# A mixture-of-experts transformer layer on one core: the turns of the expert's intermediate rows move behind the next gate/up products

## What is computed

```python
def moe(x, w_router, router_bias, w_gate, w_up, w_down, ws_gate, ws_up, ws_down):
    ...
    def body(acc, blk):
        rows, rw, e = blk
        xb = x_pad[rows]
        h = jax.nn.silu(xb @ w_gate[e]) * (xb @ w_up[e])
        yb = (h @ w_down[e]) * rw[:, None].astype(xb.dtype)
        return acc.at[rows].add(yb), None
    ...
    shared = (jax.nn.silu(xf @ ws_gate) * (xf @ ws_up)) @ ws_down
    return (acc[:T] + shared).reshape(B_, S, D)
```

## Time and profile before

| | us |
|---|---|
| median of 3 runs | 1646.05 (1645.39 to 1646.52) |
| the profiled execution's own time | 1649.41 |
| its span (first to last instruction) | 1647.7 |
| PE busy / PE weight loads busy | 1581.6 / 1313.5 |
| DVE busy | 1188.3 |
| ACT busy | 1031.8 |
| POOL busy | 508.1 |

### The profile page before, as it was taken

How to read it: one execution, slowest core, us unless ns; L and a number is a source line. 1 busy time by engine, 2 the same in 40 slices (tenths; PEclk the granted TensorE clock), 3 DMA queues, 4 the chain that set the end, 5 groups by cost and what they waited for, 6 DMA issues and landing times.

```text
span 1647.7 us, 32186 instructions
## 1 busy us (share of the span) xinstructions
PE 1581.6 (96%) x8246; PEld 1313.5 (80%) x8247; DVE 1188.3 (72%) x2036; ACT 1031.8 (63%) x1705; POOL 508.1 (31%) x495
## 2 busy tenths in 40 slices
PE   6999999999999999899999999999999999999985
PEld 6897888888887788778878888788888887888763
DVE  4214777777777788837777787767777787888857
ACT  3214666666666654427677777666776777778744
POOL 0000000000000135432544465543454444453426
PEclk9999999999999999899999999999999999999995
DMA  7223322222223534568999999999998999999976
GB/s 243 91 80 91 71 49 67 58 64 70 49 66 106 181 119 168 194 203 291 331 297 313 300 366 360 330 288 266 327 322 271 303 348 315 362 366 366 366 242 249
DMA packets 161319, 368.63 MB, mean 224 GB/s; under 512 B 53008, under 2 KB 73488, under 8 KB 161264
## 3 DMA queue, kind: packets, MB, share of 16 engines
q1 hardware_dynamic: 136272, 284.21, 49.4%
q0 software_dynamic: 24992, 83.73, 19.5%
HBM read 294.39 MB, written 65.11 MB: 218 GB/s over the span
## 4 chain that ended last, share of the span: by engine, by line
PE 73%; DVE 7%; DMA 7%; issue 5%; ACT 3%; ACTq 2%; POOL 1%; SPq 0%; DVEq 0%; POOLq 0%
PE bank L1024 6%; PE bank L1030 6%; PE bank L1027 6%; DMA sums_scratch<-ys,sidx 6%; PE q_ps L91 4%; PE q_ps L93 4%; PE q_ps L92 4%; PE out_ps L915 4%; PE k_ps L893 4%; PE out_ps L1083 3%; PE out_ps L1084 3%; PE q_ps L1014 3%; PE k_ps L1051 2%; PE k_ps L1052 2%; PE k_ps L1059 2%
## 5 line engine op out<-in xcount | busy, mean ns | idle before, releaser
L1916 DVE TENSOR_TENSOR gu_lo<-raw_gu,gu_hi 128x1024 fp32r<-128x1024 f32 x260 | 306.4, 1220 | 26.7 <-ACT gu_hi L1395 26.5
L1395 ACT CAST gu_hi<-raw_gu 128x1024 fp32r<-128x1024 f32 x260 | 253.2, 1050 | 3.7 <-DMA raw_gu<-in_moe_w_up_dram 2.8
L1024 PE MATMUL bank<-gu_hi,xb_hi 128*128 128x512 f32 x576 | 234.3, 407 | 5.6 <-DVE gu_lo L1916 4.3
L1027 PE MATMUL bank<-gu_lo,xb_hi 128*128 128x512 f32 x576 | 228.2, 396 | 0.0
L681 POOL DMA_INDIRECT sums_scratch<-ys,sidx x63 | 123.6, 1961 | 155.4 <-DMA sums_scratch<-ys,sidx 121.5
L1916 DVE TENSOR_TENSOR dn_lo<-raw_dn,dn_hi 128x1024 fp32r<-128x1024 f32 x130 | 152.6, 1212 | 3.2 <-ACT dn_hi L1395 2.6
L1030 PE MATMUL bank<-gu_hi,xb_lo 128*128 128x512 f32 x576 | 142.7, 390 | 2.2 <-DVE xb_lo L1920 2.2
L1024 PEld LDWEIGHTS bank<-gu_hi,xb_hi 128*128 128x128 f32 x576 | 110.8, 192 | 29.2 <-issue 6.4
L1395 ACT CAST dn_hi<-raw_dn 128x1024 fp32r<-128x1024 f32 x130 | 129.9, 1051 | 5.0 <-DMA raw_dn<-in_moe_w_down_dram 5.0
L1300 ACT CAST pt_hi<-k_ps 128x512 fp32r<-128x512 f32 (+1 forms) x192 | 85.8, 482 | 75.3 <-PE k_ps L893 74.6
L612 POOL IOTA e<- 128x64 f32 x1 | 0.2, 185 | 429.0 <-DVE xs L1712 429.0
(11 more groups left out here) (305 smaller groups left out, 3982.5 us busy)
## 6 DMA issues: line engine op xcount, KB each, us to landing
raw_gu<-in_moe_w_gate_dram SPq DMA_DIRECT2D x128, 512.0 KB
raw_gu<-in_moe_w_up_dram SPq DMA_DIRECT2D x128, 512.0 KB, 9.2
raw_dn<-in_moe_w_down_dram SPq DMA_DIRECT2D x128, 512.0 KB, 9.0
wqk<-in_fox_w_in_dram SPq DMA_DIRECT2D x66, 128.0 KB, 2.5
v_scratch<-v_out SPq DMA_DIRECT2D x32, 256.0 KB, 2.8
va<-v_scratch SPq DMA_DIRECT2D x16, 512.0 KB, 4.8
fin<-sums_scratch SPq DMA_DIRECT2D x16, 512.0 KB, 8.9
xs<-in_x_dram SPq DMA_DIRECT2D x8, 512.0 KB, 7.6
```

The lines of the kernel that those rows point to most:

```text
L1024: i = pe.matmul(o3, xb_hi[s][:, c], g_hi[:, :, c], start=c == 0, stop=False, skip_group_check=True)
L1027: pe.matmul(o3, xb_hi[s][:, c], g_lo[:, :, c], start=False, stop=False, skip_group_check=True)
L1395: a.copy(hi, raw).then_inc(S[done], 1)
L1916: dve.tensor_tensor(lo, raw, hi, ALU.subtract).then_inc(S[lo_ok], 1)
```

## The change

On PE, `turn_h` moves behind `gate_up`; the wait for `h_ok` alone stays ahead of it. One wait for `ht_lo_ok` in front of `turn_h_further` goes. On ACT, `h_hi` moves behind the four `gu_hi` copies, and on DVE `h_lo` behind the first three `gu_lo` pieces.

```diff
@@ PE, expert
                 with pe.If(before_it > 0):
-                    turn_h(m - 1)
+                    pe.wait_ge(S["h_ok"], m)
                     pe.wait_ge(S["g_lo_ok"], G_PIECES * (e + 2))
                     gate_up(par, w, "rows_", m + 1)
-                    pe.wait_ge(S["ht_lo_ok"], m)
+                    turn_h(m - 1)
                     turn_h_further(xi - 1)
                     turn_next()
                     down_further(par, e + 1, xi - 1)
                 with pe.If(before_it < 1):
-                    turn_h(m - 1)
+                    pe.wait_ge(S["h_ok"], m)
                     pe.wait_ge(S["g_lo_ok"], G_PIECES * (e + 2))
                     gate_up(par, w, "rows_", m + 1)
+                    turn_h(m - 1)
                     turn_next()
@@ ACT, first_half
                     if further_too:
                         further_half(xi - 1)
-                    h_hi(m - 1)
-                    if further_too:
                         further_silu(xi - 1)
                     if pos != "last":
                         next_gate_up(m, e, par)
+                    h_hi(m - 1)
                     if further_too:
                         further_h_hi(xi - 1)
                     silu(m)
@@ DVE, expert
                 with dve.If(before_it > 0):
                     further_sum(xi - 1)
-                    h_lo(m - 1)
                     further_h(xi - 1)
                     next_weights(range(G_PIECES - 1))
+                    h_lo(m - 1)
                     further_h_lo(xi - 1)
...
                 with dve.If(before_it < 1):
+                    next_weights(range(G_PIECES - 1))
                     h_lo(m - 1)
-                    next_weights(range(G_PIECES - 1))
```

## The result

| | before | changed |
|---|---|---|
| median of three runs | 1646.05 us | **1673.12 us** (1672.22 to 1676.19) |
| ratio, with 95% interval | | 1.0166 [1.0149, 1.0182] |
| profiled execution, its span | 1649.41, 1647.7 us | 1672.22, 1670.5 us |

What follows compares the result with a forecast made beforehand. PE, 96% busy, was taken as the bound. Pairs 7.6, late experts 5.5, on-time 2.25, ends 1.6, gain -0.6 made +16.4; two clock falls made +19.8 on the 1646.05 median: 1665 us, range 1655 to 1678.

Steps and rivals of the forecast that it cites:

- The view that decided: Waits view: ACT's four register loads per two-expert pass delay h_hi some 2.1 us, making 13 experts without a block before late.
- The copy at 2.1, down at 2.7: Late expert, us after the group's first turn: ACT's h_hi copy starts at 2.1, PE's down product at 2.7 instead of 0.81.
- The late experts with a block: Six late experts with a further block behind: +1.1 us each, less 0.75 where an odd expert without blocks runs ahead.
- With 0.2 to hand down over: PE's sequencer in late experts: 0.2 us to queue down after its wait ends at 2.5, so register reads end at 5.75.
- Zero's shift of 0.25: The group's first turn comes 0.25 us earlier in the expert: 0.15 of turns and 0.10 of a slow first product.
- The 30 experts with a block before: Gain 0.02 us each, -0.6 in all, nothing lost at L1101; rival of stalls there: +9 us, 1674, chance 0.10.
- The clock: Two falls of PE's clock to half in late experts' longer stalls, 1.7 us each, +3.4; bounds 0 and 22.
- clock falls in most late experts: Rival: thirteen clock falls give 1684 us, six give 1673; chance 0.12 for more than five.
- The ends: First expert +0.5 us, last +1.1, experts 61 and 62 taken as 0 within -2 to +2; 1.6 in the sum.
- The first rival: PE's register reads stay hidden: late experts 0.75 us each, odd ones nothing, +11.4, 1657 or 1658; chance 0.22.
- What was to be seen: Signs: L1051 waits in 13 experts, 1 to 1.9 us; L1073 in 15; gate/up 0.8 after down in odd experts.
- the weight load: Down's first weight load was assumed to wait with its product; loading ahead would save up to 0.15 per restart, 4 us.

Runs made afterwards that it cites:

- e3: The changed kernel with ACT and DVE reading two of four register counts at the head of each pass, the rest behind each expert's first half: 1655.87 us, ratio 1.0071.
- e9: The changed kernel with two more, unused register reads on ACT at the head of each pair of experts: 1707.97 us, ratio 1.0351.
- e10: The changed kernel with two of PE's three register reads moved behind the turns, ahead of the waits for ho and of down: 1678.49 us, ratio 1.0171.
- e11: The changed kernel with both the later ACT and DVE reads of e3 and the moved PE reads of e10: 1662.92 us, ratio 1.0069.
- e5: The kernel before the change, with the same later register reads on ACT and DVE as in e3: 1638.03 us, ratio 0.996.
- e14: The kernel before with later ACT and DVE register reads, the same kernel as e5, run once more: 1636.45 us, ratio 0.9941.
- e2: The changed kernel with PE reading one register at an expert's head, the other two behind gate/up and its wait: 1687.76 us, ratio 1.0261.

## Why the prediction was right or wrong

- **The number** fell inside the range in part by luck. The room up to 1678 had been left for a stall at L1101 or for six falls of the clock. Neither came in the changed kernel. What filled it were costs that the prediction had too small or had not: the hand-over of down, a shift counted twice, and slow reads. The mechanism, late halves of h and reads queued behind their wait, was as predicted.
- **The view that decided** was right: the 2.1 us of "issue" on ACT. e3 removes most of it and the two late groups fall from 19.1 to -1.6 us; e9 makes it longer and they double.
- **The copy at 2.1, down at 2.7**: 2.09 and 2.68. The late experts with a block, predicted 4.35, were 4.2 without the clock.
- **"With 0.2 to hand down over"** is the term that was most too small. From down's last wait to the next gate/up I had 3.2 us; the row of L1048 against that of L1024 gives 4.3 here, of which 0.76 is the two slow reads. The 3.55 that remain are 0.35 more than I had. I took 0.2 from an odd expert in which the sequencer had been free to run; to hand over twelve products with their weights behind a wait takes 0.8 here. The 3.0 for the reads and what follows them, which no row of the prediction shows by itself, was a little too large: 2.7 without the slow reads (933.3 to 936.80, less 0.76).
- **Zero's shift of 0.25 was taken off too often.** It has two parts, 0.10 of a slow first product and 0.15 of turns. For a late or odd expert without a block behind it I compared up to the next gate/up product, which in the kernel before has those same two turns ahead of it. So 0.15 was counted twice, in 14 experts of the middle: some 2 us. The odd expert shows it: zero to gate/up 4.69 against 4.6, yet a loss of 0.77 to 0.97 against 0.6. For experts with a block behind, where I compared up to L1073 or L1083, the same step was right: 0.25 in most of the nine.
- **Slow reads** were not thought of. Expert 12 lost 2.39 and expert 46, with a read of 772 ns, 2.11. The other part of the late group was 0.70 to 1.12 where 0.35 had been predicted: 0.15 and 0.35 of the two points above, and 0.1 because the first product behind a gap is itself slow (0.49 us at 936.80 and 1176.46, against 0.40 for the one at 1163.38 in the earlier trace rows).
- **The 30 experts with a block before**: next to nothing lost at L1101 (two waits, 0.8 us), as taken. Of the gain of 0.6 us only 0.1 is seen. 1.58 from turn to product, to the digit. e9 shows that the bound of 0.3 was no invention: 10.1 us appear there once ACT is later.
- **The clock**: two falls for 3.4 were forecast; four stretches came, at 1.4 each instead of 1.7, 5.7 in all. The rival "clock falls in most late experts" did not come true in the changed kernel (three of the thirteen). It did in e9, with falls in all six late experts with a block; in e10 there were five such experts and in e11 three.
- **The ends**: experts 0 and 1 lost 2.5 and not 1.1 (0.5 and, for expert 1 as an odd one, 0.6); 61 and 62 gave 2.5 back, just outside the -2 to +2. The last stretch gained 2.7 where a loss of 1.1 had been added. These two rows, first of the kernel before, then of the changed one, show why:

```profile
1602.00:1649.00 47.00, 28.11 (x57) 16.12 (x56) 32.51 (x45) 17.74 (x29) 28.03 (x12) 0.50 0.62 246
```

```profile
1649.00:1670.00 21.00, 0.39 (x2) 0.00 (x0) 18.28 (x15) 3.07 (x6) 8.15 (x4) 0.50 0.43 171
```

Before, 28.11 us of PE's work at the end ran at the lower clock; after, 0.39 and a stretch of 3.4 us at 1611.4. The last fall came 47 us later in this profile, 21 us later when counted from the start of the last expert, and this hides part of the loss in the pair. It is scatter and not the change's doing as far as the runs show: e5 and e14, the same kernel, differ by 13 us in this (1597.8 and 1610.9).
- **The first rival** ("reads stay hidden") falls by the 17 waits of L1024 for "issue" and by e2 and e10, in which the odd experts' loss goes away as soon as the reads go elsewhere.
- **What was to be seen**: L1051 waits 9 times and not 13. The prediction's 13 contradicted its own count, since six of the 13 late experts have a block behind them and wait at L1073: there 16, predicted 15. The waits of L1051 are 0.5 to 1.4 us where 1 to 1.9 had been named, the shorter ones behind an odd expert; the idle time before gate/up in the odd experts is 0.64 where 0.8 had been.
- On the weight load: at 932.58 the first load of down's weights and its product start together, behind a wait of 1.39 us. The Trainium skill, "TensorE: Matmul & The Clock Gate", section "Architectural detail: the array is 16× 32×32, not 1× 128×128", says that PE can pull weight loads ahead of products in flight. At 932.58 none was in flight (the last turn had ended at 931.19), so this row does not test it. At 926.60 before the turns were in flight, and load and product start 0.03 apart: there the trace does not bear it out. The prediction's 4 us for this should read 3.5 (23 times 0.15).

## What to carry to other kernels

Before you move a short step that others wait for behind a long one on the same engine, find when the long one ends against the moment the waiting engine arrives, in the worst kind of iteration and not the average one. Whatever stands behind the new wait on the waiting engine's sequencer (register reads above all) gets longer by it too: count up to the next product that is delayed, between like points. And look first at what makes the engine late: here a small edit that puts off two of four register reads gained 0.4 to 0.6%, where moving other work around them lost 1.7%.

## What the runs showed of the hardware

- **Register reads vary.** The line of PE's read of `further`, first of the kernel before, then of the changed one (min/median/max in ns):

```profile
L1169 PEldq TENSOR_LOAD <-further x64: 296/301/398, 753.3 to 1572.3; - x64
```

```profile
L1169 PEldq TENSOR_LOAD <-further x64: 296/303/952, 751.2 to 1600.1; - x64
```

The median is the same, the tail is not: over the three lines, 3 of 192 reads are above 450 ns before and 14 after. But the tail varies in any case: the other profiles with 192 such reads have 4 to 11, and e5 and e14, the same kernel, 6 and 9. That the change brings slow reads is not shown.
- **The clock does not follow the length of one wait.** In the changed kernel it fell in the late experts 6, 22 and 42, whose waits of L1073 are 2.16, 2.18 and 1.28 us, and not in 44 and 30, with 2.14 and 1.57. In e11 the same six experts wait 0.84 to 0.96, and it fell in 6, 22 and 42 again; in e3, with 0.24 to 0.95, in none. What brings it down here stays open. A wait of 1 to 2 us in an otherwise busy stretch must be reckoned with, at 1.4 us for each 3.4 at the lower level.
- **Waits that come once.** In e10 and e11, expert 1, the first odd one, stood still for 3.5 and 3.2 us in the middle of down (L1052), with nothing to wait for in the trace, and lost 5.0 and 8.65 in all (in e11 with another 1.9 at L1024). Both have the extra branch on PE. In both waits (778.2 to 781.6 and 781.7 to 784.8 us) the transfer view shows one packet of the queue that it names "q8 instruction", of 16 KB. All other kernels move one like it between 764 and 769 us, without such a wait of PE. That PE waited for instructions would fit this; no run tests it, and it stays open.
